# Loading the first projection slot between the two ada pairs, and projecting in chunks

## What is computed

```
mod_l = silu(c) @ ada_w[l] + ada_b[l]         # six parts of 1024: shift, scale, gate, twice
ul = rmsnorm(hl) * norm_g * (1 + sc1) + sh1   # latent tokens, modulated by c
uc = rmsnorm(hc) * norm_g * (1 + csc1) + csh1 # context tokens, modulated by c_ctx
pl, pc = ul @ w_in[l], uc @ w_in[l]           # one combined input projection, 2832 columns
```

## Time and profile before

| | |
|---|---|
| median of three runs | 2134.93 us |
| profiled execution, first to last instruction | 2134.6 us (the page gives no other time of it) |
| TensorE busy | 2069.5 us, 97% |
| VectorE busy | 1562.4 us, 73% |
| ScalarE busy | 1145.3 us, 54% |
| DMA over the span | 470.12 MB, mean 220 GB/s |
| mean granted TensorE clock | 0.994 |

### The profile page before, as it was taken

How to read it: one execution, slowest core, us unless ns; L and a number is a source line. 1 busy time by engine, 2 the same in 40 slices (tenths; PEclk the granted TensorE clock), 3 DMA queues, 4 the chain that set the end, 5 groups by cost and what they waited for, 6 DMA issues and landing times. The chain is left out here.

```text
span 2134.6 us, 35815 instructions
## 1 busy us (share of the span) xinstructions
PE 2069.5 (97%) x14756; PEld 1715.8 (80%) x14756; DVE 1562.4 (73%) x2151; ACT 1145.3 (54%) x1532; POOL 143.1 (7%) x118
## 2 busy tenths in 40 slices
PE   8999889999999999998998899999999999999997
PEld 5887777888888888877877799788888888888886
DVE  4546755889567555446466667699999999999998
ACT  4253433333432222244544345588888888888886
POOL 0013520000000000000045100100000000000000
PEclk9999999999999999999999999999999999999999
DMA  6700033454155545413000544599999999999994
GB/s 266 269 22 2 3 123 156 178 217 175 62 222 196 198 191 193 169 62 119 21 1 4 219 178 158 207 399 378 377 379 378 396 374 385 379 380 382 373 421 198
DMA packets 68485, 470.12 MB, mean 220 GB/s; under 512 B 7712, under 2 KB 8672, under 8 KB 14048
## 3 DMA queue, kind: packets, MB, share of 16 engines
q1 hardware_dynamic: 62464, 441.62, 53.5%
q10 hardware_dynamic: 4704, 21.98, 2.7%
q0 software_dynamic: 1152, 4.19, 0.5%
HBM read 455.15 MB, written 12.62 MB: 219 GB/s over the span
## 5 line engine op out<-in xcount | busy, mean ns | idle before, releaser
L2487 DVE TENSOR_TENSOR wsp_l<-ring,wsp_h 128x1024 fp32r<-128x1024 f32 x528 | 643.0, 1224 | 47.9 <-ACT wsp_h L1595 10.5
L1595 ACT CAST wsp_h<-ring 128x1024 fp32r<-128x1024 f32 x528 | 555.0, 1054 | 135.8 <-PE bank L729 79.8
L727 PE MATMUL bank<-wsp_h,xTs_h 128*128 128x512 f32 x704 | 278.6, 396 | 1.3 <-DVE wsp_l L2487 1.3
L729 PE MATMUL bank<-wsp_h,xTs_l 128*128 128x512 f32 x704 | 274.5, 390 | 0.0
L728 PE MATMUL bank<-wsp_l,xTs_h 128*128 128x512 f32 x704 | 274.3, 390 | 0.0
L2117 ACT CAST dsp_h<-ring 128x1024 fp32r<-128x1024 f32 x66 | 69.2, 1048 | 244.4 <-PE bank L1470 172.8
L3087 DVE TENSOR_TENSOR dsp_l<-ring,dsp_h 128x1024 fp32r<-128x1024 f32 x66 | 80.9, 1226 | 145.9 <-ACT dsp_h L2117 145.5
L1363 PE MATMUL bank<-u_hi,gsp_h 128*128 128x512 f32 (+1 forms) x512 | 174.1, 340 | 0.0
L1363 PE MATMUL bank<-x_lo,gsp_h 128*128 128x512 f32 (+1 forms) x512 | 172.1, 336 | 0.0
L1363 PE MATMUL bank<-u_hi,gsp_l 128*128 128x512 f32 (+1 forms) x512 | 172.1, 336 | 0.0
L2393 DVE SCALAR_TENSOR_TENSOR products<-ring,cond_rows 128x1024 bf16<-128x1024 f32 x128 | 156.5, 1223 | 4.7
(11 more groups left out here) (402 smaller groups left out, 4086.8 us busy)
## 6 DMA issues: line engine op xcount, KB each, us to landing
ring<-in_moe_tiles_dram SPq DMA_DIRECT2D x264, 1024.0 KB, 7.3
ring<-in_ada_tiles_dram SPq DMA_DIRECT2D x48, 1024.0 KB, 4.8
ring<-in_ffn_tiles_dram SPq DMA_DIRECT2D x33, 1024.0 KB, 6.9
ring<-in_gate_tiles_dram SPq DMA_DIRECT2D x32, 1024.0 KB, 6.9
ring<-in_in_tiles_dram SPq DMA_DIRECT2D x22, 1024.0 KB, 4.8
arena<-in_branch_tiles_dram ACTq DMA_DIRECT2D x8, 1024.0 KB, 7.5
ring<-in_out_tiles_dram SPq DMA_DIRECT2D x8, 1024.0 KB, 4.7
x_rows<-arena SPq DMA_DIRECT2D x1, 3584.0 KB, 16.2
```

The costliest lines, as they stand in the source:

```text
L727: pe.matmul(o, xTs[0][:, kk, :], whi[:, k, :], start=(kk == 0), stop=False)
L729: mm = pe.matmul(o, xTs[1][:, kk, :], whi[:, k, :], start=False, stop=(kk == KD - 1))
L1595: act.copy(wsp[0][:, g % 4, :], half_slot(MOE0, g)).then_inc(s.gq_o.up, 1)
L2487: v.tensor_tensor(wsp[1][:, g % 4, :], half_slot(MOE0, g), wsp[0][:, g % 4, :], ALU.subtract).then_inc(s.gq_pt.up, 1)
```

## The change

The order of the loads becomes: ada tiles 0 and 1, first projection slot, ada tiles 2 and 3, second projection slot, ada tiles 4 to 7. Two numbers without a transfer (`HELD`, n = 10 and 11) are put into the list, so that the third and fourth projection slots go to the buffers of ada tiles 4 and 5 and wait for these, not for the first two projection slots.

On TensorE the first products of slot 0 (chunks 0 and 1) stand ahead of pair 1; ScalarE casts the part of the weights that they need by itself (512 columns, a signal of its own, `first_hi`). Chunks 2 to 7 take turns in banks 4 and 5 for the transposes, where chunks 2 to 5 had banks of their own (`chunk_bank`), so chunks 4 and 5 are transposed only after chunks 2 and 3 are evacuated. The columns of pair 1 follow directly behind its products, ahead of the transposes of chunks 4 and 5. `first_part(i, ks)` projects single chunks of slot i. The halves are cast in the order first slot, second slot, second half of the second slot, second half of the first.

```diff
-            return k if k < 6 else k - 2
+            return k if k < 2 else 4 + k % 2
...
-            for n, (src, shape) in enumerate(slots):
+            first = ADA_SLOT[0:2] + WIN_SLOT[0][0:1] + ADA_SLOT[2:4] + WIN_SLOT[0][1:2]
+            for n in first + list(range(len(first), len(slots))):
+                if n in HELD:
+                    sp.wait_ge(slot_full[n % RING], 16)
+                    sp.sem_inc(slot_full[n % RING], 16)
+                    continue
...
                     prenorm_T(s, (2, 3))
-                    ada_pair(1)
-                    prenorm_T(s, (4, 5))
-                    ada_columns(1, 7, 2)
...
-                        begin(0, 0)
                         first_products()
-                        input_half(0, c0, 0, 0, (2, 3))
+                        ada_pair(1)
+                        ada_columns(1, 7, 2)
+                        prenorm_T(s, (4, 5))
+                        first_part(0, (2,))
+                        first_part(0, (3,))
+                        first_part(1, (0,))
                         ada_pair(2)
-                        begin(1, 2)
-                        input_half(1, WIN[0][0][1], 2, 0, (0, 1))
+                        first_part(1, (1,))
                         ada_columns(2, 7, 2)
+                        first_part(1, (2,))
+                        first_part(1, (3,))
+                        prenorm_T(s, (6, 7))
                         ada_pair(3)
-                        prenorm_T(s, (6, 7))
+                        first_part(1, (4, 5))
                         ada_columns(3, 7, 2)
-                        input_half(1, WIN[0][0][1], 2, 0, (2,))
-                        input_half(0, c0, 0, 1)
-                    else:
-                        input_half(1, c0, 2, 0, (3,))
-                        input_half(1, c0, 2, 1)
+                        first_part(0, (4, 5))
+                        first_part(0, (6, 7))
+                        first_part(1, (6, 7))
...
                     for j in range(PAIRS):
-                        if j == 2:
-                            act.wait_ge(*s.w_used(1))
-                            weight_high(2)
                         ada_copy(j, 6, 2 * j + 2)
-                        if j == 1:
-                            weight_high(0)
+                        if j == 0:
+                            act.wait_ge(slot_full[WIN_SLOT[0][0] % RING], 16)
+                            act.copy(win_hi[0][:, 0:2 * CW], ring[:, WIN_SLOT[0][0] % RING, 0:2 * CW]).then_inc(first_hi, 1)
...
                         input_high(2 * j + 1)
+                        if j == 0:
+                            act.copy(win_hi[0][:, 2 * CW:], ring[:, WIN_SLOT[0][0] % RING, 2 * CW:D]).then_inc(s.w_hi.up, 1)
                         if j == 1:
                             weight_high(1)
+                        if j == 2:
+                            weight_high(2)
+                            act.wait_ge(*s.w_used(1))
+                            weight_high(3)
```

More of the change, by code:

```diff
@@ L372, in build_program @@
                     ada_slots(EARLY[4:8])
+                    HELD = list(range(len(slots), len(slots) + 2))
+                    slots += [None, None]
             GATES.append(len(slots))
@@ L416, in win_half @@
             if l == 0 and i < 2:
-                return 2 * half + i
+                return 3 - i if half else i
             return 2 * i + half - 2 * (i > AB_AT)
@@ L857, in first_products, with first_part, input_half @@
                                       start=False, stop=False)
[L859 removed]
+                def first_part(i, ks):
+                    half = ks[0] // 4
+                    q = win_half(0, i, half)
+                    pe.wait_ge(*s.w_lo(q + 1))
+                    pe.wait_ge(*s.x_lo(ks[-1] + 1))
+                    w = [win_hi[win_buffer(0, q)], ring_lo[:, WIN_SLOT[0][i] % RING, D * half:D * (half + 1)]]
+                    for m in range(2):
+                        for k in ks:
+                            c = CW * (k % 4) + P * m
+                            for p, (x, u) in enumerate(((0, u_hi), (0, x_lo), (1, u_hi))):
+                                mm = pe.matmul(bank[2 * i + m][:, :], w[x][:, c:c + P], u[:, k, :],
+                                               start=(k == 0 and p == 0), stop=(k == KD - 1 and p == 2))
+                        if ks[-1] == KD - 1:
+                            mm.then_inc(s.win_mm.up, 1)
+                    if ks[-1] == 3:
+                        mm.then_inc(s.w_used.up, 1)
+                    if ks[-1] == KD - 1:
+                        pe.wait_ge(*s.win_mm(2 * i + 2))
+                        pe.sem_inc(s.w_used.up, 1)
+                        pe.sem_inc(slot_free, 1)
+                def input_half(i, c0, unit, half):
                     q = win_half(l, i, half)
[L862 removed]
                     low = ring_lo[:, WIN_SLOT[l][i] % RING, :]
@@ L867, in input_half @@
                     if c0 < OFF_Z or c0 == OFF_F:
[L868 to L879, removed]
+                        for m in range(2):
+                            for k in range(4 * half, 4 * half + 4):
+                                if i == 0 and m == 0:
+                                    pe.wait_ge(*s.x_lo(k + 1))
+                                a = CW * (k % 4) + P * m
+                                for p, (x, u) in enumerate(((0, u_hi), (0, x_lo), (1, u_hi))):
+                                    mm = pe.matmul(bank[(unit + m) % 4][:, P * toks[0]:TOK], w[x][:, a:a + P],
+                                                   u[:, k, P * toks[0]:TOK],
+                                                   start=(k == 0 and p == 0), stop=(k == KD - 1 and p == 2))
+                            if half:
+                                mm.then_inc(s.win_mm.up, 1)
                     else:
@@ L891, in input_half @@
                                 mm.then_inc(s.win_mm.up, 1)
-                    if half == 0 and (not chunks or 3 in chunks):
+                    if half == 0:
                         mm.then_inc(s.w_used.up, 1)
@@ L2643, in _ @@
                 step = 0
-                for q in range(1 if l else 3, 16):
+                for q in range(1 if l else 4, 16):
                     weight_low(q)
-                    if q == 3:
+                    if q == (3 if l else 4):
                         v.wait_ge(prm_in[l], 32 + 16 * l)
```

43 lines of the change are left out of this document (22 added, 21 removed).

## The result

The changed kernel takes 2142.1 us (median of six runs, 2140.76 to 2142.98), the kernel before 2134.91 us beside it (six runs, 2132.72 to 2139.2). The ratio is 1.0029, with a 95% interval of 1.0018 to 1.004: slower by 3.8 to 8.5 us. The forecast of 2139.8 us, which is +4.9 us, lies in that interval; the median lies in the range of 2136.0 to 2142.3, close to its upper end. The profiled execution has a span of 2140.9 us, against 2134.6 before, and its own time is 2142.74 us.

A forecast was written before the change was run, and what follows sets the result against it. The prediction took TensorE to bound the kernel, with head delays passing whole to the end: 3.2 us from steps 1 and 2 plus 1.7 us for one clock fall, 4.9 us, gave 2139.8 us, range 2136.0 to 2142.3.

The forecast's parts named there:

- What bounds the head: Head of the kernel: TensorE, busy for 97% of the span; a delay of the head passes whole to the end.
- Step 1: Head up to chunk 2 of the first slot: its first product starts at 28.3 instead of 25.21 us, 3.1 us later.
- Step 2: From chunk 2 to the third slot: changed waits bring the sum to +3.2 us, third slot at 55.5 instead of 52.30.
- step "-0.16": Third slot's first product: earlier load removes its wait for low weights, 0.46 us, leaving 0.30 us for TensorE's own matmuls.
- step "+1.0": Chunks 6 and 7 of the first slot: a new wait on TensorE for chunk 7's low part, +1.0 us.
- What was cost at nothing: Head: reordered casts and subtractions of weight halves, third slot's cast, moved loads on SP and the ring's turn add 0 us.
- Step 3, the clock: TensorE's new idle gaps between 17.25 and 27.0 us make the granted clock fall; each fall costs 1.7 us.
- forecast of one fall: Head: the clock falls once behind the new gaps, costing 1.7 us; chance 0.42.
- The sum: Whole kernel: 3.2 + 1.7 = 4.9 us, added to the median before, gives 2139.8 us.
- The rival without a fall: Head: gaps too short or broken by other work, so only 3.2 us are left, 2138.1 us; chance 0.28.
- that with two falls: Head: one clock fall for each of two idle stretches, 3.4 us in all, 2141.5 us; chance 0.18.
- the absorbed case: Behind the head: a load-ended wait takes up TensorE's delay, giving 2134.9 us or a little less; chance 0.12.

The follow-up runs named there:

- the mixed order: Changed kernel with loads and start as in the kernel before, its mixed chunks and early load kept: 2135.65 against 2137.31 us for the kernel before, ratio 0.9994.

## Why the prediction came out as it did

- *What bounds the head*: right. A delay of 4.5 to 4.7 us at the third slot moved the median by 4.6 us, with an interval of 2.8 to 7.0, and what the distance loses between 240 and 320 us it loses in kernels without a delay too.
- *Step 1*: right, and closely: first product 19.35 forecast and 19.41 measured, pair 1 22.3 and 22.34, columns 24.7 and 24.76, transposes 27.0 and 26.93, chunk 2 28.3 and 28.39. Each of these instants came from durations of the kernel before, laid one behind the other.
- *Step 2*: steps 1 and 2 together were right (+3.2 at full clock, +3.4 measured in the kernel with filled gaps), but not every term of step 2 was, and that the errors are small and partly cancel is luck. Pair 2 takes 1.94 us instead of 2.59, as forecast. The step "-0.16", the early load of the third slot, failed: the load alone moved nothing (0.46 us before and after). I had taken the 0.30 us of another boundary for the floor of this one, which has one more semaphore instruction, 0.15 us, in TensorE's queue. The load itself was issued at 35.44 in the changed kernel, 9.3 us sooner than at 44.73 and not 18. The step "+1.0" was put down as idle time; 0.74 us of it is idle by the trace, and taking the late columns out gives 1.0 us back in all. What was cost at nothing cost nothing: no wait for a weight half shows on TensorE from 19 to 57 us.
- *The split between loads and order* was not worked out in the prediction, and in the experiments my first idea of it was wrong: along the path taken, the order of loads, pair 1's place and the columns' place take about a third each. From the mixed order the loads take more, so the shares belong to the path and not to the parts.
- *Step 3, the clock*: right in the mechanism and in the price of a fall, 1.7 us, which came from the earlier trace rows. The forecast of one fall held in the profiled execution, but it isn't a property of the kernel: the repetition had two. That the bare gaps bring the falls is shown by the fillers: in the four profiles with bare gaps (the changed kernel twice, pair 1 ahead, the loads alone) the clock falls in the head, in the four with the gaps filled it stays at 1.00 from 16 to 60 us. The Trainium skill, "TensorE: Matmul & The Clock Gate", section "Why this matters for your kernels", warns of idle gaps longer than any that stand here. The traces don't bear that length out as a limit, since the clock fell behind a single gap of 2.10 us, and behind gaps of 1.52 and 1.29 us with work between.
- *The sum*: 4.9 us forecast, 5.26 us measured at the third slot with one fall, 6.4 us with two (58.91 against 52.48), and a ratio of 1.0029 or 1.0026, which is 6.2 or 5.6 us. The forecast is on the low side of both, as it counts one fall for every execution. The rival without a fall came true only with fillers, that with two falls in the repetition; the absorbed case is refuted by the added delay.

What stays open: which executions get one fall in the head and which two, and how often. The distance of 6.3 us between the two profiled spans is not the head's 5.26 us carried through: it is 3.2 us from 320 to 950 us, and falls that differ behind the head bring it to 6.2 by 1200. The profile of the changed kernel lost 6.8 us of full-speed time from 1182 to 1208 us, that of before none. The repetition of the changed kernel lost none there either, and that of before lost 3.4 us from 1178 to 1186, so this is the chance of an execution and not the change.

## What to carry to other kernels

Before a transfer is moved ahead of another one, follow the chain behind the transfer that now comes later: work that could be done sooner is worth nothing if it had filled the very wait that stays. Price a new gap on TensorE twice, by its own length and by the fall of the clock behind it, and the second only where TensorE is the bound. Before a wait is booked as a gain, move what it is said to wait for and see whether it shrinks: the releaser that a profile names is inferred. Where a change is worth 0.2%, compare instants of the same instruction at milestones; times of whole runs tell no parts apart.

## What was not expected of the hardware

- Falls of TensorE's clock come in pieces of 1.7 us of full-speed time or multiples of it, away from the kernel's end (1.70, 1.72, 3.42 and 6.82 by stretches of 2 us in these traces), and one kernel has them in different places in different executions: at 143 us in one profile of the kernel before and not in the other, behind the gap of 2.1 us in one execution of the changed kernel and not in the other.
- Useless matmuls in a gap made the head faster by 1.8 us (57.56 to 55.73); in layer 1 they brought back 6.8 us of clock and 0.4 us of time (977.87 to 977.48).
- Three semaphore instructions in TensorE's queue, with no data missing, hold the first product of a slot for 0.46 us, two for 0.30: 0.15 us apiece.
